# Two-layer block, second layer: eight projection blocks as four pairs of seven block products

## What is computed

```python
h = _rmsnorm(x, norm_w)
u = (h @ w_in).astype(f32)
gla_u, rwkv_u = u[..., :GLA_IN], u[..., GLA_IN:]
gq, gk, gv, glr, gg = _split(gla_u, GLA_SPLITS)
log_a = jax.nn.log_sigmoid(glr @ gla_gate_up.astype(f32) + gla_gate_bias.astype(f32)) / GLA_TAU
...
o = _gla_chunked(q, k, v, log_a.reshape(B, T, GLA_HEADS, GLA_DK))
...
gla_out = o.reshape(B, T, GLA_VW) * jax.nn.silu(gg)
rg = rwkv_u[..., RWKV_SHIFT_W:]
...
rwkv_out = (y + bonus.reshape(B, T, RWKV_W)) * jax.nn.silu(rg)
merged = jnp.concatenate([gla_out, rwkv_out], axis=-1).astype(x.dtype)
return x + merged @ w_out
```

## Time and profile before

| | |
|---|---|
| median of 3 runs | 2258.57 us (2257.77 to 2260.57) |
| span of the profiled execution | 2256.0 us |
| PE busy | 2151.3 us, 95% |
| DVE busy | 1583.8 us, 70% |
| ACT busy | 1007.4 us, 45% |
| POOL busy | 631.9 us, 28% |

### The profile page before, as it was taken

The page is one execution under the profiler, slowest core; times in us unless marked ns, Lnnn a source line. Parts: engine busy times, 40 slices in busy tenths (PEclk is TensorE's granted clock), DMA queues, the critical chain, the costliest instruction groups (busy, mean ns, idle before and its releaser), DMA issues. The chain is left out here.

```text
span 2256.0 us, 45654 instructions
## 1 busy us (share of the span) xinstructions
PE 2151.3 (95%) x19036; PEld 1439.9 (64%) x19036; DVE 1583.8 (70%) x2072; ACT 1007.4 (45%) x1778; POOL 631.9 (28%) x405
## 2 busy tenths in 40 slices
PE   7999999999999899899999999999999999989998
PEld 4666665566666566567888885448644445568857
DVE  6875897988888755877888884246788676236654
ACT  3226766666666543544444443235553332224321
POOL 3455674210001220054333331000154533101160
PEclk9999999999999999999999999999999999999999
DMA  3113323677777632211111214326424532033422
GB/s 134 47 42 92 93 59 83 137 139 144 146 143 143 136 106 76 99 42 52 57 59 60 61 49 177 103 68 207 135 82 142 157 105 81 23 98 100 168 62 75
DMA packets 291189, 224.64 MB, mean 100 GB/s; under 512 B 204512, under 2 KB 254880, under 8 KB 289584
## 3 DMA queue, kind: packets, MB, share of 16 engines
q1 hardware_dynamic: 290992, 221.83, 36.3%
HBM read 148.86 MB, written 28.86 MB: 79 GB/s over the span
## 5 line engine op out<-in xcount | busy, mean ns | idle before, releaser
L1506 DVE TENSOR_TENSOR_SCAN att_left<-att_left,att_unseen_prefix 16x16 f32<-16x16 f32 (+5 forms) x144 | 184.3, 1281 | 33.0 <-ACT att_left L1345 32.9
L2990 PE MATMUL ps<-second_x_hi,whi_z 128*128 128x512 f16 (+1 forms) x480 | 179.0, 373 | 3.4 <-POOL wlo_z L2955 1.9
L1239 PE MATMUL ps<-x_hi,whi_z 128*128 128x348 f16 x560 | 175.5, 313 | 3.4 <-DVE att_q L1450 3.4
L2991 PE MATMUL ps<-second_x_lo,whi_z 128*128 128x512 f16 (+1 forms) x480 | 178.7, 372 | 0.0
L2992 PE MATMUL ps<-second_x_hi,wlo_z 128*128 128x512 f16 (+1 forms) x480 | 178.7, 372 | 0.0
L1241 PE MATMUL ps<-x_hi,wlo_z 128*128 128x348 f16 x560 | 174.4, 312 | 0.0
L1240 PE MATMUL ps<-x_lo,whi_z 128*128 128x348 f16 x560 | 174.3, 311 | 0.0
L2955 POOL TENSOR_TENSOR wlo_z<-wraw_z,whi_z 128x1024 f16<-128x1024 f32 x28 | 65.8, 2349 | 181.2 <-ACT whi_z L3183 181.2
L1465 DVE SCALAR_TENSOR_TENSOR att_left_split<-att_left,att_left_split 128x256 f16<-128x256 f32 (+7 forms) x128 | 106.2, 830 | 7.3 <-ACT att_left_split L1359 7.3
L1359 ACT ACTIVATE att_left_split<-att_left 128x256 f16<-128x256 f32 (+7 forms) x128 | 86.8, 679 | 36.6 <-DMA att_left_turned<-att_left_split 29.0
L1345 ACT ACTIVATE att_left<-ps 16x16 f32<-16x16 f32 (+5 forms) x144 | 86.0, 597 | 36.6 <-PE ps L1255 36.3
(11 more groups left out here) (680 smaller groups left out, 6695.2 us busy)
## 6 DMA issues: line engine op xcount, KB each, us to landing
wraw_z<-in_w_second SPq DMA_DIRECT2D x30, 512.0 KB, 3.7
wraw_z<-in_w_up SPq DMA_DIRECT2D x26, 512.0 KB, 3.7
wraw_z<-in_w_qkv SPq DMA_DIRECT2D x24, 512.0 KB, 4.5
wraw_z<-in_w_down SPq DMA_DIRECT2D x20, 512.0 KB, 3.7
raw_down<-in_w_down SPq DMA_DIRECT2D x20, 512.0 KB, 4.4
seg<-dt_a_sums SPq DMA_DIRECT2D x18, 512.0 KB, 5.2
wraw_z<-in_w_up SPq DMA_DIRECT2D x36, 256.0 KB, 2.6
second_work<-parked_units SPq DMA_DIRECT2D x7, 1280.0 KB, 6.5
```

Of the source, the lines that this page charges most:

```text
L1239: nc.tensor.matmul(lin_ps(g), hi, xhi, start=(kb == 0), stop=False)
L1506: nc.vector.tensor_tensor_scan(x, x, unseen, 1.0, ALU.mult, ALU.max).then_inc(s_scan, 1)
L2990: nc.tensor.matmul(out, hi, xhi, start=(j == 0), stop=False)
L2991: nc.tensor.matmul(out, hi, xlo, start=False, stop=False)
```

## The change

**Seven products.** Blocks 22 to 29 become four pairs. Pair i takes blocks 22 + 2i and 23 + 2i as the rows, and the two halves of the inputs as the columns, of a 2 by 2 block matrix of weights (A11, A12, A21, A22); the tokens 0 to 511 and 512 to 1023 and the two halves of the inputs give the 2 by 2 matrix of the input. In place of eight block products it makes seven (P1 to P7), in Winograd's form, of 4 x 3 matmuls of 512 columns each. It needs four sums of weight blocks for each pair (S1 to S4, POOL's `combine`) and four sums of input blocks (T1 to T4, of 4 x 512 columns each), made once. The four quarters of the result are put together by ACT (`keep`, three evictions to `seven_kept`) and DVE (`quarter`, three additions), and ACT applies `silu` in three further steps (`gated_out`).

**Input sums.** Round r, 0 to 3: four additions on POOL restore f32 inputs from their parts (`whole_inputs`), DVE makes four differences and, after ACT's four copies (`t_highs`), four low parts (`t_differences`). They stand in the steps of blocks 14 to 17, at the places that the fences below show. The sums are held in `t_hi` and `t_lo`.

**Weights of the pairs.** The loads come as quarter, whole and quarter; POOL no longer scales or cuts blocks 22 to 29, ACT makes seven high parts for a pair with the scale in it (`part_high`), DVE seven low parts (`part_low`). S1 to S4 as cut are kept in the part of `second_x_hi` and `second_x_lo` that only block products of the ordinary kind would still read. The products' order is P1, P2, (middle of a block), P6, P5, (end of a block), P7, (middle), P3, P4, (end), with the units' work of two blocks at the places in brackets. Two stores of the inverses move behind the last load.

```diff
+SEVEN0 = UNIT0
+SEVENS = (SECOND_B - SEVEN0) // 2
+ORDER_2 = ("P1", "P2", "P6", "P5", "P7", "P3", "P4")
+SPLITS_2 = ("A11", "A12", "S2", "S1", "S3", "A22", "S4")
+T2_AT = {GLA0 + 1: (0,), GLA0 + 2: (1, 2), GLA0 + 3: (3,)}
...
+        t16 = [ctx.enter_context(nc.sbuf_tensor(n, [P, 4, DB // 2, BANK], F16)) for n in ("t2_hi", "t2_lo")]
+        kept = ctx.enter_context(nc.sbuf_tensor("seven_kept", [P, 3, BANK], F32))
...
-                for i in range(SLOTS, SECOND_B):
+                for i in range(SLOTS, SEVEN0):
...
-                    if i == G0 + 1:
-                        sp.wait_ge(s_inv, 1)
...
+                for i in range(SEVENS):
+                    g, u = L.w[SEVEN0 + 2 * i], L.w[SEVEN0 + 2 * i + 1]
+                    if i == 0:
+                        sp.wait_ge(L.cut, SEVEN0 - 1)
+                    else:
+                        sp.wait_ge(s_slo, split_low(i - 1, "S3"))
+                    sp.dma_start(s32["A11"], half(g, 0)).then_inc(s_in["A11"], 16)
...
+                def whole_inputs(r):
+                    if r == 0:
+                        pool.wait_ge(s_mixed, GLA0)
+                        pool.wait_ge(s_fin, RWKV_P)
+                    elif r >= 2:
+                        pool.wait_ge(s_tlo, tlo(r - 2))
+                    for t, (k, h) in zip(t_temps(r), ((r, 1), (r, 0), (r + DB // 2, 1), (r + DB // 2, 0))):
+                        cols = slice(h * BANK, (h + 1) * BANK)
+                        nc.gpsimd.tensor_tensor(t, S.xhi[:, k, cols], S.xlo[:, k, cols], ALU.add).then_inc(s_tsum, 1)
+                def combine(i):
+                    pool.wait_ge(s_in["U"], in_(i, "U"))
+                    pool.wait_ge(s_in["A11"], in_(i, "A11"))
+                    if i:
+                        pool.wait_ge(s_slo, split_low(i - 1, "S1"))
+                    nc.gpsimd.tensor_tensor(s32["S1"], s32["A21"], s32["A22"], ALU.add).then_inc(s_comb, 1)
+                    pool.wait_ge(s_comb, combined(i, 1))
+                    nc.gpsimd.tensor_tensor(s32["S2"], s32["S1"], s32["A11"], ALU.subtract).then_inc(s_comb, 1)
+                    pool.wait_ge(s_comb, combined(i, 2))
+                    pool.wait_ge(s_slo, split_low(i, "A11"))
+                    nc.gpsimd.tensor_tensor(s32["S3"], s32["A11"], s32["A21"], ALU.subtract).then_inc(s_comb, 1)
+                    pool.wait_ge(s_in["A12"], in_(i, "A12"))
+                    pool.wait_ge(s_slo, split_low(i, "A12"))
+                    nc.gpsimd.tensor_tensor(s32["S4"], s32["A12"], s32["S2"], ALU.subtract).then_inc(s_comb, 1)
...
+                    for r in T2_AT.get(j, ()):
+                        whole_inputs(r)
...
+                def block_product(i, name, out, of, start, end):
+                    pe.wait_ge(s_slo, split_low(i, name))
...
+                def seven(i):
+                    j = SEVEN0 + 2 * i
+                    if i == 0:
+                        pe.wait_ge(s_out, SEVEN0 - 1)
+                    elif i >= 2:
+                        pe.wait_ge(s_c21, SEVEN0 + i - 1)
+                    block_product(i, "A11", bank_a(i), x_of(0, 0), True, False)
+                    if i == 0:
+                        pe.wait_ge(s_out, SEVEN0)
+                    else:
+                        pe.wait_ge(s_quarter, nth_quarter(i - 1, "C11"))
+                    block_product(i, "A12", bank_b, x_of(0, DB // 2), True, True)
+                    amid(j)
+                    if i == 0:
+                        pe.wait_ge(s_tlo, tlo(DB // 2 - 1))
+                    pe.wait_ge(s_kept, nth_kept(i, "P1"))
+                    block_product(i, "S2", bank_a(i), t_of(2), False, False)
+                    if i:
+                        pe.wait_ge(s_quarter, nth_quarter(i - 1, "C12"))
+                    block_product(i, "S1", bank_c, t_of(1), True, False)
+                    behind(j)
+                    pe.wait_ge(s_kept, nth_kept(i, "U2"))
+                    block_product(i, "S3", bank_a(i), t_of(3), False, False)
+                    amid(j + 1)
+                    pe.wait_ge(s_kept, nth_kept(i, "P5"))
+                    block_product(i, "S4", bank_c, x_of(1, DB // 2), False, True)
+                    pe.wait_ge(s_quarter, nth_quarter(i, "C22"))
+                    block_product(i, "A22", bank_a(i), t_of(4), False, True)
+                    behind(j + 1)
...
+                def t_highs(r):
+                    for n, (t, m) in enumerate(((1, 1), (0, 3), (2, 2), (3, 4))):
+                        act.wait_ge(s_tdiff, tdiff(r, n))
+                        nc.scalar.activation(t16[0][:, m - 1, r, :], t_temps(r)[t], ACT.Copy).then_inc(s_thi, 1)
...
+                def part_high(i, name):
+                    if i == SEVENS:
+                        return
+                    if name[0] == "A":
+                        act.wait_ge(s_in[name if name[1] == "1" else "U"], in_(i, name))
+                    else:
+                        act.wait_ge(s_comb, combined(i, int(name[1])))
+                    if i:
+                        act.wait_ge(s_p, free(i - 1, name))
+                    else:
+                        act.wait_ge(s_lin, SEVEN0 - (name in ("A11", "A12")))
+                    nc.scalar.activation(w16[0][name], s32[name], ACT.Copy, scale=WSCALE).then_inc(s_shi, 1)
...
+                def gated_out(i):
+                    act.wait_ge(s_p, made(i, "P4"))
+                    nc.scalar.activation(c21(i), bank_a(i), ACT.Silu, scale=1.0 / WSCALE).then_inc(s_c21, 1)
+                    act.wait_ge(s_quarter, nth_quarter(i, "C12"))
+                    nc.scalar.activation(c22(i), c22(i), ACT.Silu)
+                    nc.scalar.activation(place(SEVEN0 + 2 * i), place(SEVEN0 + 2 * i), ACT.Silu)
...
+                    for r in {GLA0 + 2: (0,), GLA0 + 3: (1, 2), GLA0 + 4: (3,)}.get(j, ()):
+                        t_highs(r)
...
+                def t_differences(r):
+                    now = t_temps(r)
+                    dve.wait_ge(s_tsum, tsum(r))
+                    for n, (out, x, y) in enumerate(((1, 0, 1), (0, 2, 0), (2, 2, 1), (3, 3, 2))):
+                        if n:
+                            dve.wait_ge(s_tdiff, tdiff(r, n - 1))
+                        nc.vector.tensor_tensor(now[out], now[x], now[y], ALU.subtract).then_inc(s_tdiff, 1)
+                    for n, (t, m) in enumerate(((1, 1), (0, 3), (2, 2), (3, 4))):
+                        dve.wait_ge(s_thi, thi(r, n))
+                        nc.vector.tensor_tensor(t16[1][:, m - 1, r, :], now[t], t16[0][:, m - 1, r, :], ALU.subtract).then_inc(s_tlo, 1)
+                def part_low(i, name):
+                    if i == SEVENS:
+                        return
+                    dve.wait_ge(s_shi, split_high(i, name))
+                    nc.vector.scalar_tensor_tensor(w16[1][name], s32[name], WSCALE, w16[0][name], ALU.mult, ALU.subtract).then_inc(s_slo, 1)
+                def quarter(out, of, add):
+                    nc.vector.scalar_tensor_tensor(out, of, 1.0 / WSCALE, add, ALU.mult, ALU.add).then_inc(s_quarter, 1)
...
+                t_differences(0)
...
                 gate(nc.vector.scalar_tensor_tensor(low, gx, -1.0, gx, ALU.mult, ALU.min))
+                for r in range(1, DB // 2):
+                    t_differences(r)
...
+                for name in SPLITS_2:
+                    part_low(0, name)
+                for i in range(SEVENS):
+                    c = 2 * i
+                    if i:
+                        part_low(i, "A22")
+                        part_low(i, "S4")
+                    part_low(i + 1, "A11")
+                    dve.wait_ge(s_p, made(i, "P2"))
+                    dve.wait_ge(s_kept, nth_kept(i, "P1"))
+                    if i >= (G0 - SEVEN0) // 2:
+                        dve.wait_ge(s_inv, 1)
+                    quarter(c11(i), bank_b, p1)
+                    unit_front(c)
+                    if i:
                         unit_squares(c - 1)
+                    part_low(i + 1, "A12")
+                    unit_state(c)
+                    part_low(i + 1, "S2")
+                    part_low(i + 1, "S1")
+                    dve.wait_ge(s_p, made(i, "P7"))
+                    dve.wait_ge(s_kept, nth_kept(i, "P5"))
+                    quarter(c22(i), bank_a(i), p5)
+                    unit_front(c + 1)
+                    dve.wait_ge(s_p, made(i, "P3"))
+                    dve.wait_ge(s_kept, nth_kept(i, "U2"))
+                    quarter(c12(i), bank_c, u2)
+                    unit_squares(c)
+                    part_low(i + 1, "S3")
                     if c in rest:
                         substitute(*rest[c])
-                    if there(c):
-                        unit_state(c)
+                    unit_state(c + 1)
+                    if c + 1 in rest:
+                        substitute(*rest[c + 1])
+                unit_squares(NUNIT - 1)
```

139 lines of the change are left out of this document (108 added, 31 removed).

## The result

The changed kernel takes 2281.1 us (median of 4 runs, 2279.3 to 2281.5) against 2259.0 us of the kernel before on the same chip; ratio 1.0094, 95% interval 1.0081 to 1.0106. It is 0.9% slower. The prediction said 2280 (2262 to 2292). The profiled execution has a span of 2279.2 us, 23.2 more than before. The trace tells how much of this is the path that was predicted.

What follows compares the result with a forecast made beforehand. PE's matmuls were taken to bound the projection blocks. A 28.1 us delay, less 10.4 saved, plus 0.5 for evictions and 3.0 for the clock, gave +21.2: forecast 2280 us, range 2262 to 2292.

Steps and rivals of the forecast that it cites:

- The gain of 48 products, 10.4 us: Second layer's projection blocks: 336 matmuls instead of 384 on PE, at 0.216 us each, save 10.4 us if PE never waits.
- The cut behind the substitution: Pair 0's first low part on DVE queues behind substitution rows 15 to 18: first product 7.1 us later.
- POOL's old share: Time that POOL's scaling and cuts, now gone, had cost DVE between the gate and the first pair: 5.0 us.
- rival 3: All rounds of input sums fit in DVE's idle 25.0 us, so its chain does not move: 2253 us; chance 4%.
- The sums on DVE's chain, with turns: DVE and POOL take turns on input sums, making the gate's exponential and logarithm 23.4 us late, first low part 28.1.
- Rival 1: DVE's operations slip into POOL's gaps and only 6.6 us of queueing remain: 2260 to 2266 us; chance 20%.
- PE's waits ahead of pair 0: PE waits for late weight parts before the pairs, 5 + 4 + 4 + 5 us, all inside the 28.1 us delay.
- Pairs without waits: In the first pair DVE's 26.4 us of work fits PE's 28.2 with 1.8 to spare; no wait taken.
- rival 2: The pairs wait as well, each of the four losing 3 us: 2292 us; chance 15%.
- ACT at the end, +0.5: At the end ACT has three evictions instead of one before the sums' eviction: 0.5 us more.
- SP's stores: Two stores of the inverses move behind the last weight load, some 28 us before the end: no cost.
- Clock, +3.0: After ten idle us before pair 0, PE runs at half clock for a while: 3.0 us more.

Runs made afterwards that it cites:

- kernel 1: Changed kernel without the input sums, the block products reading constants instead; 2261.1 us, ratio 0.9999 to the kernel before.
- Kernel 5: Changed kernel with pair 0's seven low parts ahead of substitution rows 15 to 18 on DVE; 2280.1 us, ratio 1.0084 to the kernel before.
- kernel 2: Changed kernel with POOL's 16 input-sum additions over 8 columns in place of 512; 2273.1 us, ratio 1.0059 to the kernel before.
- kernel 11: Kernel before with 178 more already-met wait instructions on PE ahead of the last phase; 2284.2 us, ratio 1.0095 to the kernel before.
- kernel 3: Changed kernel with the last phase's 4 MB load of the parked hidden state cut in two; 2278.3 us, ratio 1.0083 to the kernel before.
- kernel 4: Changed kernel with 78 more already-met wait instructions on PE ahead of pair 0; 2276.3 us, ratio 1.0074 to the kernel before.
- kernel 6: Changed kernel with the gate's exponential and logarithm ahead of ACT's copies of rounds 1 to 3; 2278.7 us, ratio 1.0077 to the kernel before.
- kernel 7: Changed kernel with input-sum rounds 0 and 1 and round 2's additions moved into the RWKV blocks; 2267.4 us, ratio 1.0043 to the kernel before.

## Why the prediction was right, step by step

- **The gain of 48 products, 10.4 us**: right. The stretch from the first pair product to the last phase shortened by 8.0: to 0.1, the 10.4, less 2.9 of clock, and 0.6 at the joint. The 216 ns per product held in the pairs too.
- **The cut behind the substitution**: right in kind. 4.15 us by kernel 1, for a step put at 7.1, or at 4.6 without POOL's old share (rival 3's sum). Kernel 5, which takes the rows away beside the sums, gives 5.5.
- **The sums on DVE's chain, with turns**: right in mechanism, too dear in size. The gate's chain was said to be 23.4 us late; its step came at 1843.42, 19.6 late. The term that was too large is an addition on POOL: 1.25 us was taken from a row with two f32 inputs, and with its two f16 inputs it took 1.12. And a turn is shorter than the sum of both operations: beside each other, an addition and a DVE operation pass in 1.57, not in 1.25 + 0.68 = 1.93. The Trainium skill (SBUF — State Buffer, SBUF: two separate sides) says that the one that starts first holds the shared ports for its whole instruction while the other is fully blocked; that gives 1.12 + 0.68 = 1.80 for the pair, and the rows show 1.57, so the blocking is real here but some 0.2 us of the two lie over each other. The first pair product was 23.6 late in place of 28.1, a miss of 4.5 us. Additions of 1.9 us and more where they meet DVE, named as a sign, did not come: beside differences they took 1.6, and only the one beside the gate's second step took 3.2. Rival 1 (turns cost little) is refuted by kernel 2: they are worth at least 7.6.
- **PE's waits ahead of pair 0**: 5 + 4 + 4 + 5 were said, 1.8 + 4.0 + 1.3 + 2.9 came; low part 17 ended at 1819.7, said 1821.6. The wait for pair 0 was 9.4 ("some ten"). They were not the last, as said.
- **Pairs without waits** (against rival 2): right, with the small reserve that was named; kernel 5 shows that 5.5 us more on DVE are enough to break it.
- **ACT at the end, +0.5**: ACT's evictions cost 0.28 (PE's wait 1.06 in place of 0.78), and the joint as a whole gained 0.6. **SP's stores**: nothing, as said. **Clock, +3.0**: right, 2.9.
- **What was not foreseen**: the 6.6 us in the last phase. With it left out, the sum would have given 23.6 - 8.0 = +15.6 and a time near 2274, still slower. The predicted 2280 is so close to 2281.1 because a term that was 4.5 us too large, another of 1.1 at the joint, and two that were missing, 6.6 in the last phase and 1.0 ahead of block 15, nearly cancel. The verdict and its main cause hold by the experiments; the last 7 us of agreement are luck.

Open is which of the boundaries beside the load gets the long pause, and why the packet starts late there: whether it stands behind the 4 MB load or is asked for late. What is shown is that 78 instructions on PE without any work decide over the hole, and that the pauses stand at every 256th instruction. Open too are the 1.6 us of the last phase that lie ahead of the hole. The Trainium skill (SBUF — State Buffer, SBUF: two separate sides) states that a DMA and a compute operation cannot slow each other. No run here measures that for operands; the changed kernel and kernel 11 show PE standing still beside a load all the same, behind a late load of its own instructions, and by kernels 3 and 4 the size of the load and the number of instructions ahead of it decide over that.

## What to carry to other kernels

Before counting a saved product as a gain, list what the helper engines must add for it, and ask for each operation whether its chain has room at that place: an engine at 80% may have none, and an idle stretch that the new work fills with two engines at once loses what their turns take. Sums that depend only on the stage's input belong where their chain is waited for by nobody; of the two rounds that were moved into the RWKV blocks here neither had such a place, and PE waited 2.7 and 2.9 us behind them. When a phase that was not edited changes by some us, look for idle stretches of PE released by "issue" beside a large load, count at which instruction they stand, and shift that count by some tens of empty instructions before explaining the time in any other way.

## What the runs showed of the hardware

- An addition of two f16 inputs into f32, 128 x 512, on POOL took 1.12 us alone and 1.57 beside DVE; DVE's difference of two f32 inputs of that size took 0.68 alone, 1.53 beside such an addition and 2.5 to 2.6 beside POOL's cut of 128 x 1024 (2.1 us alone).
- All pauses of PE above 0.3 us without a wait in the last phase stood at a multiple of 256 instructions from each other (33 in fourteen traces, two of them one off) and ended 1.3 to 1.7 us behind a 16 KB packet of instructions. Beside a 4 MB load (share 1.0 of the DMA engines) the changed kernel and kernels 1, 2, 5, 6 and 7 had one of 2.5 to 3.4 us, in the changed kernel with six us at half clock behind it: the last phase took 266.3 to 268.6 us in place of 259.7. With a 2 MB load the longest there was 0.9 us and the clock stayed.
- A wait of 1.8 us ahead of block 17 left the clock at 1.00. An idle stretch of 3.2 us in the pairs was followed by eight us at half clock, and two of 1.26 and 1.06 us close together by three at 0.65 on average.
- An instruction of PE that only waits for what is already met cost 96 ns (178 of them 17.0 us); two waits went into one (156 made 78).
- The first 1790 us were passed up to 5 us sooner or later from one kernel to another. Counted from a common product, the first pair product of kernels 3 and 4, whose edits leave it alone, agreed with the changed kernel's within 0.02 us; the first 250 products of the last phase, the same code in all, took 16.1 to 19.4 us.
